# Router logits taken from w_out's output block by block, one-pass normed tokens, single-pass position and table matmuls, and 1 MB expert loads

## What is computed

```python
yl = m @ w_out                                                  # 512 x 2048
xl = xl + mod_l[2] * yl
hl2 = rmsnorm(xl, norm2_w) * (1 + mod_l[4]) + mod_l[3]
scores = sigmoid(hl2 @ w_router)                                # 512 x 16
sel = scores + router_bias                                      # best group of 4, best 2 in it
gate = gate / sum(gate)
# tokens sorted by expert into blocks of 128 rows, each block with the weights of one expert
yb = (silu(xblk @ w1[e]) * (xblk @ w3[e])) @ w2[e]
f  = at each token: the sum of its two rows of yb, times gate
xl = xl + mod_l[5] * f
return rmsnorm(xl, final_norm_w)
```

## Time and profile before

| what | us |
|---|---|
| median of 3 runs | 2496.8 (2493.49 to 2497.17) |
| the profiled execution's own time | 2496.68 |
| its span (first to last instruction) | 2495.1 |
| until the merge ends, about | 1518 |
| w_out's stage, four blocks | 1529.9 to 1718.7 |
| from there to the first expert matmul | 1718.7 to 1811.5 |
| expert stage | 1811.5 to about 2435 |
| tail | to 2495.1 |

### The profile page before, as it was taken

The page is one execution under the profiler, slowest core; times in us unless marked ns, Lnnn a source line. Parts: engine busy times, 40 slices in busy tenths (PEclk is TensorE's granted clock), DMA queues, the critical chain, the costliest instruction groups (busy, mean ns, idle before and its releaser), DMA issues.

```text
span 2495.1 us, 34704 instructions
## 1 busy us (share of the span) xinstructions
PE 2221.1 (89%) x10837; PEld 1815.6 (73%) x10837; DVE 1586.5 (64%) x1886; ACT 980.4 (39%) x1186; POOL 610.5 (24%) x698
## 2 busy tenths in 40 slices
PE   2679999999999998999999998986699999999990
PEld 1169888888888885877777876775677777777770
DVE  2076645666566564765666665335479999989984
ACT  3044422333233333222222222222167777777771
POOL 0025514543445343111111111001002122121222
PEclk9889999999999999999999998998589999999995
DMA  9945422222222223667777766441589999999985
GB/s 373 417 132 167 145 85 81 84 81 77 81 86 78 84 75 94 219 214 225 226 224 236 231 193 237 146 125 47 189 300 366 392 367 379 383 379 378 384 328 219
DMA packets 386603, 532.11 MB, mean 213 GB/s; under 512 B 15072, under 2 KB 261344, under 8 KB 379008
## 3 DMA queue, kind: packets, MB, share of 16 engines
q1 hardware_dynamic: 353216, 392.93, 46.0%
q0 software_dynamic: 33344, 138.63, 15.9%
HBM read 494.77 MB, written 36.73 MB: 213 GB/s over the span
## 4 chain that ended last, share of the span: by engine, by line
PE 72%; DVE 6%; issue 4%; DMA 2%; ACT 2%; POOL 1%; ACTq 0%; SPq 0%; POOLq 0%; DVEq 0%
PE ps L624 12%; PE ps L626 12%; PE ps L625 12%; PE ps L888 5%; PE ps L890 5%; PE ps L889 5%; DVE e_lo L1790 3%; PE ps L795 2%; PE ps L838 2%; PE ps L839 2%; PE ps L796 2%; PE ps L797 2%; PE ps L840 2%; PE ps L684 2%; DMA e_raw<-in_w_e 1%
## 5 line engine op out<-in xcount | busy, mean ns | idle before, releaser
L1362 DVE TENSOR_TENSOR w_lo<-raw,w_hi 128x1024 fp32r<-128x1024 f32 x272 | 351.2, 1292 | 413.3 <-ACT w_hi L1006 413.1
L1790 DVE TENSOR_TENSOR e_lo<-e_raw,e_hi 128x1024 fp32r<-128x1024 f32 x384 | 500.6, 1326 | 64.0 <-ACT e_hi L1233 52.4
L1006 ACT CAST w_hi<-raw 128x1024 fp32r<-128x1024 f32 x272 | 284.6, 1047 | 643.9 <-PE ps L626 321.8
L624 PE MATMUL ps<-hl_hi,w_hi 128*128 128x512 f32 x1280 | 509.2, 398 | 0.5 <-DVE s_ctx L1435 0.5
L626 PE MATMUL ps<-hl_hi,w_lo 128*128 128x512 f32 x1280 | 499.3, 390 | 0.0
L625 PE MATMUL ps<-hl_lo,w_hi 128*128 128x512 f32 x1280 | 499.2, 390 | 0.0
L1233 ACT CAST e_hi<-e_raw 128x1024 fp32r<-128x1024 f32 x384 | 400.1, 1057 | 166.9 <-PE ps L890 117.6
L626 PEld LDWEIGHTS ps<-hl_hi,w_lo 128*128 128x128 f32 x1280 | 240.9, 188 | 50.9
L624 PEld LDWEIGHTS ps<-hl_hi,w_hi 128*128 128x128 f32 x1280 | 241.2, 188 | 49.8 <-issue 1.7
L625 PEld LDWEIGHTS ps<-hl_lo,w_hi 128*128 128x128 f32 x1280 | 241.2, 188 | 49.1 <-issue 1.7
L888 PE MATMUL ps<-e_hi,xe_hi 128*128 128x512 f32 x512 | 207.8, 406 | 35.5 <-DVE e_lo L1790 32.6
(11 more groups left out here) (323 smaller groups left out, 3561.5 us busy)
## 6 DMA issues: line engine op xcount, KB each, us to landing
e_raw<-in_w_e SPq DMA_DIRECT2D x384, 512.0 KB, 7.1
raw<-in_w_in SPq DMA_DIRECT2D x208, 512.0 KB, 3.7
ada<-in_w_ada POOLq DMA_DIRECT2D x64, 1024.0 KB, 5.9
ada_ring<-in_w_ada SPq DMA_DIRECT2D x16, 2048.0 KB, 17.0
raw<-in_w_out SPq DMA_DIRECT2D x32, 512.0 KB, 4.8
block_outputs<-y_sb POOLq DMA_DIRECT2D x32, 512.0 KB
raw<-in_w_branch_pool SPq DMA_DIRECT2D x16, 512.0 KB, 3.9
raw<-in_w_branch_hgrn SPq DMA_DIRECT2D x16, 512.0 KB, 4.0
```

Of the source, the lines that this page charges most:

```text
L624: mm(dst, hi, rhs_hi[:, k, :], start=(k == 0), stop=False)
L1006: act_e.copy(w_hi[:, hslot, :], raw[:, slot, :]).then_inc(hi_done, 1)
L1362: tt(w_lo[:, hslot, :], raw[:, slot, :], w_hi[:, hslot, :].bitcast(F32), ALU.subtract).then_inc(split_done, 1)
L1790: tt(e_lo[:, hslot, :], e_raw[:, slot, :], e_hi[:, hslot, :].bitcast(F32), ALU.subtract).then_inc(e_split, 1)
```

## The change

- **Logits.** DVE takes a tile's bank as soon as that tile's last matmuls of the block are done (`w_mm`), not the whole block's. `x2` of a finished block, unnormed, is transposed during the next block (`turn_x2`, 16 transposes a block) and multiplied with `w_scaled` = router weights times (1+m4)*norm2, in four matmuls of 32 rows beside each other in PE's columns (`part_logits`); at the end four small matmuls add the four groups, DVE scales by the token's root and adds `m3_logit`. The squares of a block move to ACT's turn in the next block. `h2T`, its copies and the 64 fp32 logit matmuls are gone.
- **Normed tokens.** During the next block DVE makes `h2 = x2 * ((1+m4)*norm2)` (`modulated`); at the end one pass a tile (`normed`): tile 0 before the logits, tile 1 beside the sigmoid, tiles 2 and 3 behind the gates. POOL no longer takes part.
- **Positions and table** in fp32r: 5 matmuls for 14 and 8 single ones for 8 that took two passes.
- **Expert stage.** Row p*16+k (w2: p*4+k) on partition p, so a load is 1 MB with 8 KB in one piece on each partition; six raw slots of 1 MB; six split slots, `AHEAD = 5`; the first five casts stand before `table_rdy`. The transposes of `xe` and `act` read every 16th and every 4th column for it. POOL stores the result as ACT copied it; `m5_row` comes in at the tail.
- **Tail.** ACT scales `y0`; DVE makes a weighted sum, a product with `m5_row` and a sum with `x2`: three operations a tile for two.
- PE's three last blocks of w_out are written out instead of looped; one more vector load (`norm2_w`) and two small strided ones (`m34_col`) are added, the 1 MB load of `m4_row` goes.

```diff
-    w_e1_d = w_e1[0].rearrange("e (k p) n -> e p k n", p=P)
+    w_e1_d = w_e1[0].rearrange("e (p k) n -> e p k n", p=P)
...
+            def piece(e, n):
+                w, k, rows = (w_e1_d, n, 4) if n < 4 else (w_e3_d, n - 4, 4) if n < 8 else (w_e2_d, n - 8, 1)
+                return w[ds(e, 1), :, rows * k:rows * k + rows, :].rearrange("o p k n -> (o p) (k n)")
+            for n in range(8):
+                if n == 2:
+                    sp.wait_ge(x2_rdy, 20)
+                if n == 3:
+                    sp.wait_ge(part_mm, 4)
+                if n == 4:
+                    sp.wait_ge(h2_rdy, NTOK)
+                if n == 5:
+                    sp.wait_ge(y_out, 16 * NTOK)
+                if n == 6:
+                    sp.wait_ge(xe_in, 16)
+                load_e(n, n % EP, piece(0, n))
...
+            def part_logits(cb):
+                pe.wait_ge(x2T_rdy, X2T + cb * 4 + 4)
+                pe.wait_ge(ws_rdy, cb + 1)
+                for j in range(4):
+                    last = mm(ps[32 * j:32 * j + 32, 6, :], w_scaled[:, j, :], x2T[:, j, :], start=(cb == 0),
+                              stop=(cb == 3), tile_position=(0, 32 * j))
...
+                        if u == 7 and t < NTOK - 1:
+                            last.then_inc(w_mm, 1)
...
+                    if cb and u in (1, 2):
+                        turn_x2(cb - 1, 2 * u - 2)
+                        turn_x2(cb - 1, 2 * u - 1)
+                    if cb and u == 4:
+                        part_logits(cb - 1)
...
                 for j in range(4):
                     last = pe.transpose(ps[:, 6 + part % 2, j * P:(j + 1) * P],
-                                        xe[:, (4 * part + j) * P:(4 * part + j + 1) * P], ident[:])
+                                        xe[:].rearrange("t (p k) -> t k p", k=KT)[:, 4 * part + j, :], ident[:])
...
-            AHEAD = 3
-            act_e.wait_ge(table_rdy, 1)
-            for q in range(AHEAD):
-                e_hi_unit(q, q, q, 16)
+            AHEAD = EH - 1
+            for q in range(AHEAD):
+                e_hi_unit(q, q, 16 * (q // 2 // EP + 1))
+            act_e.wait_ge(table_rdy, 1)
...
+            for i in range(NTOK):
+                act_e.wait_ge(y_in[i], 32)
+                activate(y0[:, i, :], y0[:, i, :], ACT.Copy, scale=gate_w[:, 0, i:i + 1]).then_inc(y0_rdy, 1)
...
                 for t in range(NTOK):
+                    if t < NTOK - 1:
+                        dve.wait_ge(w_mm, cb * 3 + (t + 1))
+                    else:
+                        dve.wait_ge(units_done, cb * 8 + (2 + S_W + 8))
+                    tt(x2[:, t, at(512)], bank(t), m2_part[:], ALU.mult).then_inc(w_ev, 1)
+                    if t:
+                        add_x(t - 1)
+                add_x(NTOK - 1)
...
-                dve.wait_ge(y_in[i], 32)
-                step(stt(out=o, in0=y0[:, i, :], scalar=gate_w[:, 0, i:i + 1], in1=x2[:, i, :], op0=ALU.mult,
-                         op1=ALU.add))
-                stt(out=o, in0=y1[:, i, :], scalar=gate_w[:, 1, i:i + 1], in1=o, op0=ALU.mult, op1=ALU.add
-                    ).then_inc(f_sum, 1)
+                dve.wait_ge(y0_rdy, i + 1)
+                step(stt(out=o, in0=y1[:, i, :], scalar=gate_w[:, 1, i:i + 1], in1=y0[:, i, :], op0=ALU.mult,
+                         op1=ALU.add))
+                step(tt(o, o, m5_row[:], ALU.mult))
+                tt(o, o, x2[:, i, :], ALU.add).then_inc(f_sum, 1)
...
                     pool.wait_ge(y_ev, b * 4 + (6 + 2 * n))
-                    own.did(tt(y_sb[:, cols], y_sb[:, cols], m5_row[:, cols], ALU.mult))
-                    own.wait()
                     pool.dma_start(y_d[ds(b * BLK, BLK), cols], y_sb[:, cols]).then_inc(y_out, 16)
```

More of the change, by code:

```diff
@@ L555, in _ @@
                     e = sp.value_load(route_i[0:1, ds(b, 1)], min_val=0, max_val=E - 1)
[L556 to L558 removed]
+                    for n in range(12):
+                        load_e(b * 12 + (E * 12 + n), n % EP, piece(e, n))
                 sp.nop()
@@ L866, in _ @@
-            logits(NTOK - 1)
-            pe.wait_ge(sel_rdy, 1)
-            chosen = rt[:, 8, :].rearrange("p (t e) -> p t e", e=E)
-            for t in range(NTOK):
-                for s in range(t + 1):
-                    mm(ps[:, 1, t * E:(t + 1) * E], upper[:] if s == t else ones[:], chosen[:, s, :],
-                       start=(s == 0), stop=(s == t))
-            for s in range(NTOK):
-                last = mm(ps[:, 2, 0:E], ones[:], chosen[:, s, :], start=(s == 0), stop=(s == NTOK - 1))
+            project(1)
@@ new lines, in _ @@
+            project(2)
+            pe.wait_ge(col_rdy, COL_SUM)
+            pe.wait_ge(x2T_rdy, X2T + 8)
+            mm(bank(TR, E), ones[:], m3_part[:], start=True, stop=True).then_inc(m3_step, 1)
+            project(3)
+            for t in range(NTOK):
+                turn_x2(3, t)
+            part_logits(3)
+            pe.wait_ge(lg_step, LG_PART)
+            pe.wait_ge(col_rdy, COL_GROUPS)
+            pe.wait_ge(w_ev, 20)
+            for t in range(NTOK):
+                last = mm(ps[:, 0, t * E:(t + 1) * E], osq[:, t * P:(t + 1) * P], group_sum[:], start=True, stop=True)
@@ new lines, in _ @@
+            last.then_inc(lg_step, 1)
+            pe.wait_ge(col_rdy, COL_EXACT)
+            pe.wait_ge(sel_rdy, 1)
+            counts = ps[:, 1, 0:(NTOK + 1) * E]
+            chosen = chosen_r[:].rearrange("p t e -> p (t e)")
+            mm(counts, upper_r[:], chosen, start=True, stop=False, skip_group_check=True)
+            for s in range(1, NTOK + 1):
+                last = mm(counts[:, s * E:], ones_r[:], chosen[:, 0:(NTOK + 1 - s) * E], start=False,
+                          stop=(s == NTOK), skip_group_check=True)
@@ L1183, in merged_hi, with square, x2T_copy @@
                 act_e.copy(m_hi[:, 2 * n:2 * n + 2, :], m_sb[:, 2 * n:2 * n + 2, :]).then_inc(h_hi, 1)
+            def square(cb, prev, t):
+                act_e.wait_ge(x2_rdy, cb * 4 + (4 * prev + 4 + t + 1))
+                own.wait()
+                if isinstance(cb, int):
+                    n = cb + prev
+                    cols, one = slice(n * 512, n * 512 + 512), slice(n, n + 1)
+                else:
+                    cols, one = ds(cb * 512 + prev * 512, 512), ds(cb + prev, 1)
+                own.did(activate(bank(UB), x2[:, t, cols], ACT.Square, accum_out=part_sq[:, t, one]))
+            def x2T_copy(cb, prev, t):
+                act_e.wait_ge(x2_T, cb * 4 + (X2_T + 4 * prev + t + 1))
+                act_e.wait_ge(part_mm, cb + prev)
+                act_e.copy(x2T[:, :, t * P:(t + 1) * P], bank(4 + t % 2).rearrange("p (j t) -> p j t", j=4)
+                           ).then_inc(x2T_rdy, 1)
             def out_hi(cb, first, last):
@@ L1666, in _, with step @@
                 project(cb, False, False)
+            dve.wait_ge(m3_step, 1)
+            dve.tensor_copy(m3_logit[:], bank(TR, E)).then_inc(m3_step, 1)
             project(3, False, True)
+            R = lambda i: rt[:, i, :]
+            R3 = lambda i: rt[:, i, :].rearrange("p (t e) -> p t e", e=E)
+            R4 = lambda i: rt[:, i, :].rearrange("p (g a) -> p g a", a=4)
+            SM = lambda i: rt_small[:, i, :]
+            def step(ins):
+                own.did(ins)
+                own.wait()
+            modulated(3, 0)
+            dve.wait_ge(units_done, 2 + S_W + 32)
+            own.did(dve.tensor_copy(ones_r[:], ones[:]))
+            own.did(dve.memset(SM(15), 0.0))
+            own.wait()
+            own.did(dve.tensor_copy(chosen_r[:, NTOK, :], SM(15)))
+            dve.tensor_copy(upper_r[:], upper[:]).then_inc(col_rdy, 1)
             dve.wait_ge(sq_done, 16)
```

413 lines of the change are left out of this document (214 added, 199 removed).

## The result

The changed kernel takes 2413.1 us (median of 4 runs, 2411.4 to 2414.8), the kernel before 2495.1 on the same chip (4 runs, 2489.6 to 2497.2): a ratio of 0.9675, with a 95% interval of 0.9656 to 0.9693. The prediction was 2429 with a range of 2410 to 2463. The time lies in the range, but the gain is 82 us where 68 were forecast. Two of its terms were off by more than 4 us, in opposite directions.

A forecast was written before the change was run, and what follows sets the result against it. Bounds: a routing chain with no bounding engine, DVE and POOL excluding each other in the expert stage, DVE's queue in the tail. From 2496.68: -42.1 - 33.6 + 0.8 + 6.7 + 0.5 = -67.7, so 2429 us; range 2410 to 2463.

The forecast's parts named there:

- Routing: Last w_out matmul to first expert matmul: chain of small steps shortened to 50.6 us, 42.1 us less.
- The last step: End of the routing chain: table to first expert matmul stays as before, 13.7 us.
- Expert stage: Blocked subtractions go and PE is next; an expert takes 36.5 us instead of 38.74, 33.6 us less.
- The bound of -47: Expert stage, largest gain: 15 x 3.1 = 47 us, as 36.3 holds gaps that the modelled ends hide.
- 402 GB/s: Expert stage: DMA rate needed for 36.5 us an expert; 8 KB pieces judged nearest to ada loads at 427.
- DMA engines were the bound and stay it: Rival, expert stage: an expert stays at 38.7 us, the kernel takes 2463 us; chance 13%.
- The lock: Expert stage: DVE and POOL exclude each other at a shared SBUF port pair; 3.8 us is 1.3 + 2.4.
- The strided transposes: Expert stage, xe and act read with a step: 0 taken, other end 22 us; as rival 2451 us, 14%.
- weight loads of the xe transposes over 140 ns: Expert stage: listed among the signs in the profile that the forecast is wrong.
- w_out: w_out's stage: 9.7 us added to PE, 8.9 of waits removed, net +0.8; bounds -2 and +6.
- Tail: After the last expert: POOL's multiplications go, -4.8; ACT scaling +1.9, a DVE pass for each of four tiles; +6.7 us.
- a DMA share that falls under 1: Profile sign that the forecast is right; the DMA share before was 1.02 in the expert stage.

The follow-up runs named there:

- late kernel: Changed kernel with transposes, PSUM copies and part_logits of w_out's first three blocks moved after the last w_out matmul, wide form kept; 2417.1 us.
- mended tail: Changed kernel with ACT's squares between scalings, its root table loaded earlier, DVE's variance operation moved, GpSimd's empty turns before the last store's wait; 2404.0 us.

## Why the prediction was right, and where its steps were not

That the time lies in the range owes something to luck. The expert stage gained 15.0 us more than forecast and the tail cost 4.8 more; with the tail as forecast the kernel would take 2408 us, under the low end of 2410.

- **Routing, -42.1 forecast, -44.4 measured.** Each step came 1 to 3 us early. The squares and copies took 4.3 us instead of 5.7, since ACT's square and copy of a tile interleave (1.1 us a tile), and the choice and the positions were a little shorter. The last step was 14.5 instead of 13.7. The sum was right; what carries it was not said: the four-wide form was a line of the working (1.0 us), and the runs show it to be worth 12 to 22 us, where the place alone, with this form, is worth 2.
- **Expert stage, -33.6 forecast, -48.6 measured. This is the step that failed in size:** "PE idles 38.74 x 32.2 / 520 = 2.4 us an expert and could do one in 36.3". The floor was taken from PE's busy time, and a matmul's record (0.39) is longer than the distance to the next (0.2267), so each wait is shown too short, and matmuls that follow a wait are stretched. Counted by starts, an expert is 144 x 0.2267 = 32.64, and five groups of transposes at 0.35 to 0.39 with a next matmul 0.09 late each, 2.3, together 34.9. The rows of before had this: a group of four at 2099.44 is followed by a matmul at 2099.79. The bound of -47 for the same term, "36.3 holds gaps that the modelled ends hide", named the reason, and the measured term lies 1.6 us outside it. Also 14 periods were to be had, not 15, and their mean was 38.63: 14 x 3.54 = 49.6, less 1.0 in the first 67 us of the stage.
- The Trainium skill, page Perfetto Trace Analysis, section Identifying the Most-Contended Engine, says that matmul busy time is a poor measure of how far PE is from its limit. The trace agrees: 94% busy before (374.25 of 400), with 9% still to gain.
- **The transfers.** "402 GB/s" was reckoned to be needed and 418 were moved. The argument (8 KB pieces are nearest to the ada loads with 427) held. The rival "DMA engines were the bound and stay it" was half right: they were the next bound of the kernel before, behind the lock, at about 400 and not at 379, and would have kept 19 us of the gain back without the new layout. The Trainium skill, page DMA: Bandwidth & Descriptors, section Where 436 GB/s comes from, puts the ports' ceiling at 435 GB/s and the memory's share of one core at about 358; here one core moved 418 to 423 from memory, so the second figure is no bound for a core alone.
- **The lock** was read right: the 3.8 us subtractions went with POOL's multiplication and come back with it (3.89).
- **The strided transposes.** 0 forecast, 1 us by the periods. The step "I take nothing" held by the sum, but its reason (the slower base rate of a weight load hides the stride) did not: the loads did get longer, 140 to 194 ns, a ratio of 1.39, which is that of the moving side in the earlier trace rows. That they run beside the matmuls before them is the likely reason, which no run shows. The comparison of 0.65 with 1.1 ns a column was not sound either: it counts 2048 columns, where the earlier trace rows has 8 records of 128, 1024 columns and 1.3 ns each. And "weight loads of the xe transposes over 140 ns", named as a sign of being wrong, came with the forecast's time unharmed. The rule on lines of 16 bytes that the prediction cited from the Trainium skill (page SBUF — State Buffer, section Door 1) agrees with the record, 194 against 141 ns, and its price all but fails to reach the path.
- **w_out.** +0.8 forecast, about -1.8 within the stage (it starts 1.4 us later, with its first load landing later, and ends 0.4 earlier). The waits at block boundaries are gone and the blocks 46.6 to 46.8 us apart, just under the forecast 47 to 49. Without the added PE work they are 43.7 (late kernel): 3.2 us a block had been reckoned, and it is 3.0. What was reckoned too small is what went away: the stage takes 188.9 us before and 177.2 in the late kernel, 11.7 less, where 8.9 were forecast. The later start is not the change's doing: the kernel with contiguous transposes, the same up to there, starts at 1529.05, and that with four split units at 1533.24.
- **Tail, +6.7 forecast, +11.5 measured. This step failed:** "the last rows arrive about 10 us after the first, which DVE's nine passes cover". The fourth tile lands 15 us after the first (2378.32 against 2363.46), the square then takes 1.9 and its table load 1.28, and DVE waits 4.2. In pieces: from the last copies to the first gather 11.2 us instead of 14.7 (-3.5, forecast -4.8), from there to DVE's first pass 2.1 more (forecast 1.9), DVE's passes 12.9 more (forecast 9.6). The mended tail confirms the cause, since it takes 5.1 us out of DVE's stretch.
- Of the forecast signs of being right, "a DMA share that falls under 1" did not come: it stayed at 1.01, since the loads run ahead as far as their buffers let them. Share alone did not tell a bound from a full queue; ACT's waits for e_raw did.

## What to carry to other kernels

Take PE's floor from the distances between starts, one full round of them, and not from its busy share: here it was 34.9 and not 36.3, 1.4 us in each of 14 periods. Where PE is the bound of the stage into which work is moved, that stage gives back most of what the chain gains (9.6 of 11.7 us with the wide form); so look at the form of the work as well. Many columns moving over a small stationary tile, instead of 16 over a full one, saved time on both sides, and in the chain it went with the higher clock. And before an operation is moved off the bound engine, look at what that engine waits for: DVE had room for m5's product exactly because the operation it replaced on ACT was what DVE waited for.

## What was not expected of the hardware

- A weight load of 128 columns with a step of 4 or 16 elements takes 205 or 194 ns instead of 140, and only 3.5 ns of it reach the distance between matmuls.
- With pieces of 8 KB one core moves 418 GB/s as asked and 423 when it is the bound; with 2 KB pieces for two thirds of the bytes 402. The share of busy time shows 1.01 and 1.04.
- 16 fp32 matmuls of 16 columns take 3.64 us inside w_out at a granted clock of 1.00 and 4.8 to 7.0 in the chain, at 0.76 to 0.50. Four matmuls of 512 columns in four column groups take 1.06 in both, and in the chain the granted clock was 1.00 with them.
- After the pause of the routing the first expert matmuls run at the lower clock for 4 to 6 us in all profiled runs but one (the kernel before without the multiplications, 0.3), so up to a microsecond that comes late there is partly given back.
- Why the first 67 us of the expert stage take 1.0 us longer in the changed kernel (68.3 against 67.3) stays open; with counts and table in fp32 they took 67.3 as well.
